# Depthwise convolution: four terms of each tile computed by TensorE, three fills placed elsewhere

## The reference, cut to what matters

```python
a = h @ pw1_w + pw1_b
u, g = jnp.split(a, 2, axis=-1)
u = u * jax.nn.sigmoid(g)
u = lax.conv_general_dilated(u, dw_w[:, None, :], (1,), [(15, 15)], ..., feature_group_count=D_MODEL) + dw_b
u = (u - mean(u)) * rsqrt(var(u) + eps) * ln_g + ln_b
return silu(u) @ pw2_w + pw2_b
```

## Time and profile before

| | us |
|---|---|
| three runs, median (lowest to highest) | 3093.72 (3091.89 to 3101.62) |
| the profiled execution | 3105.27 |
| its span, from first to last instruction | 3103.2 |
| TensorE busy | 2953.2 (95%) |
| VectorE, ScalarE, GpSimd busy | 1638.8, 1289.8, 168.0 |

### The profile page before, as it was taken

The page is one execution under the profiler, slowest core; times in us unless marked ns, Lnnn a source line. Parts: engine busy times, 40 slices in busy tenths (PEclk is TensorE's granted clock), DMA queues, the critical chain, the costliest instruction groups (busy, mean ns, idle before and its releaser), DMA issues.

```text
span 3103.2 us, 50896 instructions
## 1 busy us (share of the span) xinstructions
PE 2953.2 (95%) x17586; PEld 2524.6 (81%) x17586; DVE 1638.8 (53%) x3043; ACT 1289.8 (42%) x2511; POOL 168.0 (5%) x120
## 2 busy tenths in 40 slices
PE   7999999999999999999998868999999999989998
PEld 7979789799797997788886536788878888768998
DVE  5566775565567755532326785523334333448554
ACT  4445455455454555422323443423333323335543
POOL 0000010000000100000001760000000000000000
PEclk9999999999999999999999989999999999999999
DMA  7556265565562655532324761423324333241553
GB/s 248 187 163 211 82 204 188 155 203 186 160 211 82 207 190 168 169 98 95 102 75 167 240 217 55 136 82 108 103 70 127 95 95 105 79 143 61 167 181 99
DMA packets 239196, 443.10 MB, mean 143 GB/s; under 512 B 26416, under 2 KB 27440, under 8 KB 238384
## 3 DMA queue, kind: packets, MB, share of 16 engines
q1 hardware_dynamic: 237632, 433.47, 43.7%
q0 software_dynamic: 1392, 7.34, 0.7%
HBM read 439.65 MB, written 1.05 MB: 142 GB/s over the span
## 4 chain that ended last, share of the span: by engine, by line
PE 82%; DVE 11%; POOL 2%; issue 2%; ACT 1%; DMA 1%; SPq 0%; DVEq 0%; ACTq 0%; POOLq 0%
PE ps L749 81%; DVE low L1768 2%; POOL hidden L2382 1%; DMA raw<-weights 1%; DVE hidden L1771 1%; DVE zl L1771 1%; DVE ps L1771 1%; POOL low L2352 1%; DVE x L1774 1%; DVE hidden L1768 1%; DVE coef L2305 1%; DVE zl L1768 1%; DVE hidden L2309 1%; DVE neg_max L2105 1%; DVE hidden L2132 0%
## 5 line engine op out<-in xcount | busy, mean ns | idle before, releaser
L749 PE MATMUL ps<-zh,low 128*128 128x256 f32 (+1 forms) x4192 | 1402.6, 335 | 79.4 <-DVE low L1768 37.4
L749 PE MATMUL ps<-zl,high 128*128 128x256 f32 (+1 forms) x4192 | 1382.4, 330 | 0.0
L749 PE MATMUL ps<-zh,high 128*128 128x256 f32 (+1 forms) x4192 | 1381.5, 330 | 0.0
L1768 DVE TENSOR_TENSOR low<-raw,high 128x512 fp32r<-128x512 f32 x1276 | 844.0, 698 | 439.7 <-ACT high L1308 437.8
L1308 ACT ACTIVATE high<-raw 128x512 fp32r<-128x512 f32 x1304 | 765.5, 625 | 609.2 <-PE ps L749 508.2
L749 PEld LDWEIGHTS ps<-zh,low 128*128 128x128 f32 x4192 | 806.5, 192 | 187.3 <-issue 41.5
L749 PEld LDWEIGHTS ps<-zl,high 128*128 128x128 f32 x4192 | 807.1, 193 | 72.1 <-issue 4.8
L749 PEld LDWEIGHTS ps<-zh,high 128*128 128x128 f32 x4192 | 806.8, 192 | 69.5
L1768 DVE TENSOR_TENSOR hidden<-gated,ps 128x256 f32 (+1 forms) x176 | 91.6, 520 | 603.2 <-ACT gated L1308 603.2
L1308 ACT ACTIVATE gated<-ps 128x256 f32<-128x256 f32 (+1 forms) x176 | 81.3, 462 | 493.7 <-PE ps L749 493.6
L749 PE MATMUL ps<-high,zl 128*128 128x512 f32 (+2 forms) x544 | 196.0, 360 | 3.8 <-DVE zl L1768 3.8
(11 more groups left out here) (202 smaller groups left out, 2018.5 us busy)
## 6 DMA issues: line engine op xcount, KB each, us to landing
raw<-weights SPq DMA_DIRECT2D x1642, 256.0 KB, 3.3
hidden<-norms POOLq DMA_DIRECT2D x4, 1024.0 KB, 6.4
cst<-consts SPq DMA_DIRECT2D x1, 1829.0 KB, 12.9
x<-x_in SPq DMA_DIRECT2D x1, 1024.0 KB, 6.0
x<-tokens_in POOLq DMA_DIRECT2D x1, 1024.0 KB, 12.5
x<-ctx_in POOLq DMA_DIRECT2D x1, 1024.0 KB, 6.3
out<-hidden POOLq DMA_DIRECT2D x1, 1024.0 KB, 5.1
```

Of the source, the lines that this page charges most:

```text
L749: return nc.tensor.matmul(out, lhsT, rhs, start=first, stop=last, **kw)
L1768: return nc.vector.tensor_tensor(out, a, b, op)
```

## The change

Of every tile the last 4 terms (of the last tile the last 12) go to TensorE. Their weights come as new quarters in the stream, one for four terms, each term a 128 by 128 matrix with the term's weights on its diagonal. ScalarE and VectorE make high and low parts of a window of the tile (`window_of`), in a buffer that takes the place of `h_split` in the convolution; TensorE writes the sum of its terms into the PSUM bank (`tap_product`), and VectorE then goes on adding its own terms to it. For tile 0, TensorE uses the other bank, and its sum is added to the side sum. Side products are now 7 for each tile and 5 for the last, also for tile 0; the side sum is added to VectorE's at the end, in one more instruction. GpSimd makes all low parts of the stage from the second quarter of tile 1's second half on. The convolution has 15 fills in place of 18: the first five half tiles have none behind them, and four come at the end, the last of them behind the mean in place of a `stream(12, 2)`; one fill goes behind the first block's ple, two more to the attention. The diff, cut to its core:

```diff
-SIDES = (0, 7, 9, 9, 9, 9, 9, 13)
-LATE_FILLS = 3
+SIDES = (7, 7, 7, 7, 7, 7, 7, 5)
+TAP_QUARTERS = (1, 1, 1, 1, 1, 1, 1, 3)
+LATE_FILLS = 5
 WARM = 18
 PAD = (TAPS - 1) // 2
+WINDOW = 268
...
+def conv_order():
+
+    for t in range(KT):
+        yield "up_half", t, 0
+        if t >= 3:
+            yield "fill", t, 0
+        if t >= 1:
+            yield "taps", t - 1, 0
+        yield "up_half", t, 1
+        if t >= 2:
+            yield "fill", t, 1
+    yield "taps", KT - 1, 0
+    for _ in range(4):
+        yield "fill", KT, 0
+
+
+def taps_by_pe(n):
+
+    return 4 * TAP_QUARTERS[n]
...
-        if l == DEPTH - 1:
-            yield fills.pop()
+        yield fills.pop()
...
-            for t in range(KT):
-                for a in range(2):
+            for step, t, a in conv_order():
+                if step == "up_half":
                     yield ("up_half", ("conv", 0), (t, a), 2, False)
+                elif step == "taps":
+                    yield ("taps", ("conv", 0), t, TAP_QUARTERS[t], False)
+                else:
                     yield fills.pop()
-            yield fills.pop()
-            yield fills.pop()
...
+        elif kind == "taps":
+            parts = [np.zeros((P, taps_by_pe(t), P), np.float32)]
+            parts[0][np.arange(P), :, np.arange(P)] = inp["conv_dw_w_2"][0][TAPS - taps_by_pe(t):, t * P:t * P + P].T
+            parts = [parts[0].reshape(P, -1)]
...
+        up_at, taps_at, fill_at = {}, {}, []
+        at = 0
+        for kind, key, t, n, _ in stream():
+            if kind == "up_half":
+                up_at[t] = at
+            elif kind == "taps":
+                taps_at[t] = at
+            elif kind == "ada" and up_at:
+                fill_at.append(at)
+            if key == ("pw2", 0):
+                break
+            at += n
+        pw2_at = at
...
-                if l == DEPTH - 1:
-                    self.pe.wait_ge(res_ready, 4 * DEPTH)
+                self.pe.wait_ge(res_ready, 4 * (l + 1))
+                if l == 0:
+                    self.fill(2, 3)
+                else:
                     self.fill()
...
+            def tap_product(self, n, z0):
+
+                self.pe.wait_ge(tap_low, n + 1)
+                if n == 1:
+                    self.pe.wait_ge(taps_added, 1)
+                if n >= 2:
+                    self.pe.wait_ge(z_ready, z0 + n - 1)
+                bank, last = 5 if n == 0 else 4 + n % 2, taps_by_pe(n) - 1
+                for c0 in range(0, last, 4):
+                    h, lo = self.quarter()
+                    for i in range(4):
+                        at = slice(c0 + i, c0 + i + S)
+                        w = (h[:, i * P:i * P + P], lo[:, i * P:i * P + P])
+                        m = self.mm3(ps[:, bank, :], w, (window[:, n % 2, 0, :, at], window[:, n % 2, 1, :, at]), c0 + i == 0, c0 + i == last)
+                    self.done(m)
...
-                for n in range(KT):
-                    if n >= 2:
-                        pe.wait_ge(conv_taken, seen.now(conv_taken) + n - 1)
-                    for a in range(2):
+                z0 = seen.now(z_ready)
+                steps = list(conv_order())
+                for step, n, a in steps[:-1]:
+                    if step == "fill":
+                        self.fill(6, 7)
+                    elif step == "taps":
+                        self.tap_product(n, z0)
+                    else:
+                        if n >= 2 and a == 0:
+                            pe.wait_ge(conv_taken, seen.now(conv_taken) + n - 1)
                         self.group([(ps[:, 2 * (n % 2) + g, :], True) for g in range(2)], 512, coming=coming if n == 0 else None, halves=(a,))
-                        self.fill(6, 7)
                 seen(conv_taken, KT)
-                self.fill(6, 7)
-                self.fill(6, 7)
                 for k in range(KT):
                     self.stat(512, 0, z_ready, conv_out, k)
-                self.stream(12, 2)
+                self.fill(6, 7)
...
+                    self.take_rows()
...
-                if l == DEPTH - 1:
+                if l == 0:
+                    self.fill(2, 3)
+                else:
                     self.fill()
...
-                self.act.wait_ge(quarter_done, self.q + RING)
+                self.act.wait_ge(quarter_done, up_at[n, 1] + 2 + RING)
...
+            def window_of(self, n):
+
+                self.act.wait_ge(conv_taken, self.seen.now(conv_taken) + n + 1)
+                if n >= 2:
+                    self.act.wait_ge(quarter_done, taps_at[n - 2] + TAP_QUARTERS[n - 2] + RING)
+                wide, at = S + taps_by_pe(n) - 1, TAPS - taps_by_pe(n)
+                self.f(r(window[:, n % 2, 0, :, 0:wide]), conv_in[:, n, :, at:at + wide], ACT.Copy).then_inc(tap_high, 1)
+
             def conv(self):
                 act, seen = self.act, self.seen
                 w = c("conv_w").rearrange("p (k t) -> p k t", k=KT)
-                for n in range(2):
-                    while self.s < self.q + 2:
-                        self.next_high()
-                    self.q += 2
+                fills = iter(fill_at)
+
+                def filled():
+                    self.q = next(fills)
                     self.fill(6, 7)
-                    self.next_high()
-                    self.next_high()
-                    self.q += 2
-                    self.gate_of(n)
-                    self.fill(6, 7)
-                self.next_high()
-                self.next_high()
-                for n in range(1, KT):
-                    act.wait_ge(conv_taken, seen.now(conv_taken) + n + 1)
+
+                assert self.s == up_at[1, 1] + 1
+                self.gate_of(0)
+                self.take_rows()
+                self.window_of(0)
+                for n in range(KT):
                     for t in range(SIDES[n]):
                         at = side_before[n] + t
                         if at >= 4:
                             act.wait_ge(side_added, at - 3)
                         self.f(side[:, at % 4, :].rearrange("p (a s) -> p a s", a=2), conv_in[:, n, :, t:t + S], ACT.Copy,
                                scale=w[:, n, t:t + 1]).then_inc(side_product, 1)
-                        if n == KT - 1:
-                            if t in (2, 7):
-                                self.fill(6, 7)
-                            if t == 11:
+                        if n == 0 and t < 6 or n == KT - 1 and t == 0:
+                            self.next_high()
+                        if n >= 2 and t == 0:
+                            self.take_rows()
+                        if 2 <= n < KT - 1:
+                            if t in (1, 2, 3):
+                                self.next_high()
+                            if t == 3:
+                                filled()
+                            if t == 4:
                                 self.take_rows()
-                            continue
-                        if t == 0:
-                            self.q += 2
-                            self.fill(6, 7)
-                        if t in (1, 2):
+                    if n < KT - 1:
+                        if n:
                             self.next_high()
-                        if t == 5:
-                            self.take_rows()
-                    if n < KT - 1:
-                        self.q += 2
                         self.gate_of(n + 1)
-                        self.fill(6, 7)
-                    if n < KT - 2:
-                        self.next_high()
-                        self.next_high()
+                        if n:
+                            filled()
+                            self.next_high()
+                        self.window_of(n + 1)
+                for _ in range(3):
+                    filled()
+                    self.take_rows()
+                filled()
+                assert next(fills, None) is None
+                self.q = pw2_at
                 seen(conv_taken, KT)
                 self.root_first()
                 self.ahead()
                 for k in range(0, KT, 2):
                     act.wait_ge(dev_ready, seen(dev_ready))
                     self.f(square[:, k:k + 2, :], conv_out[:, k:k + 2, :], ACT.Square).then_inc(sq_ready, 1)
+                self.take_rows()
...
-                if l == DEPTH - 1:
+                if l == 0:
+                    self.fill(2, 3)
+                else:
...
-                def next_gate(n):
-                    self.low_by_pool(2)
-                    self.q += 2
-                    self.filled()
-                    self.low_by_pool(2)
-                    self.q += 2
-                    v.wait_ge(quarter_done, self.q + RING)
-                    gate(n)
-                    self.filled()
-
-                self.used(2)
-                self.fill(6, 7)
-                self.used(2)
+                def window_of(n):
+                    wide, at = S + taps_by_pe(n) - 1, TAPS - taps_by_pe(n)
```

(121 more changed lines are left out.)

## The result

The changed kernel took **3145.38 us** (median of 4 runs, 3140.82 to 3156.31) against 3093.28: a ratio of **1.0161, interval 1.0144 to 1.0178**, or 52 us slower. One odd execution of a later kernel, 6088.39 us in the run fast_after, is left out of that kernel's ratio. The prediction said 3119, with a range of 3098 to 3132: the right sign, half the size. The profiled execution has a span of 3154.5 us against 3103.2.

The account below looks back on a forecast made before the run. TensorE was taken as the bound, busy 2953.2 of 3103.2 us, with the convolution's tiles set by a loop of fills, loads and matmuls. Terms 15.3 + 13.5 − 3.5 = +25.3 us took the 3093.72 median to 3119, range 3098 to 3132.

Parts of the forecast that it names:

- Without a price: Buffer name, pw2's layout, moved column copy and earlier row copy: no cost, under 1 us if their cover went.
- the buffer's new name: The renamed split buffer in the convolution: listed as costing nothing, under 1 us at most.
- A fill at the first block's end: After the first block's gate stage: ScalarE's high parts delay the split of x and the next FFN, +15.3 us.
- Two late fills: In attention before the scores: two more fills at 6.2 to 7.3 us each, nothing covering them, +13.5 us.
- The convolution: Whole convolution stage: earlier start and end, most given back by the fill behind the mean, −3.5 us.
- The loop: Convolution tiles 3 to 7: fill, landing, high and low parts, matmuls, next fill; 23.8 us a tile against 22.
- the wait for the side sum: Convolution's first tile: VectorE waits 4 us for GpSimd's side sum, needed before gate 1.
- the late squares: Convolution's end: ScalarE's squares wait 6 us for pw2's eighth quarter, loaded in the moved fill, delaying the second mean.
- Rival 1: Loads behind fills: the eighth is down after 7.1 us, not 10.1; +8.5 us, 3102; chance 0.12.
- Rival 2: Convolution: VectorE is the bound and gets relief, with the fills' cost −11 us, 3082.5; chance 0.15.
- Rival 3: Convolution: side products hold back low parts in every tile, +2.5 us five times; +38 us, 3132; chance 0.05.
- Rival 4: First block's end and attention: the moved fills are hidden after all; −3.5 us, 3090; chance 0.06.

Follow-up runs that it names:

- fast_after: Changed kernel, with zh, zl and the split buffer 192 bytes further in 256 column blocks and at their old place in 512 column ones: 0.9975 of the kernel before.
- shift_only: Kernel before with 384 unused bytes behind h_split and nothing else: 1.0087 of the kernel before.
- aligned: Changed kernel with 640 unused bytes behind split_buf: 3119.73 us, 1.0087 of the kernel before.
- aligned_again: The kernel of aligned run once more, beside fills_only on one chip: 1.0064 of the kernel before.
- fills_only: Kernel before with all three moves of fills, 15 left in the convolution's loop, and no tap products on TensorE: 1.0069 of the kernel before.
- ple_only: Kernel before with one fill added at the end of the first block's ple and one fewer behind the convolution's last half: 1.0031 of the kernel before.
- late_only: Kernel before with five late fills in attention for three, and the two behind the convolution's last half left out: 1.0025 of the kernel before.
- run rate: No kernel: TensorE alone, 32 products from each of 16 sources 64 bytes apart modulo 1024, then again beside other traffic: 227.5 to 233.1 ns with 512 columns.

## Why the prediction was right, and where it failed

- **The step that failed** is in the paragraph "Without a price": "the buffer's new name". It was not a new name but 96 floats more, and they moved zh and zl by 384 bytes. I had the sizes before me, priced the step under 1 us and gave no reason for it: I took an address for something without a time. It costs 27 us on the old kernel (shift_only) and 23 to 30 on the new one (1.0161 against 1.0087 and 1.0064 for aligned; 26 by the medians). The 3 × 1536 products of the three FFNs that read zh or zl, by 5.5 to 6.6 ns, are 25 to 30.
- **A fill at the first block's end, +15.3:** measured 15.4 and 15.6, and 14.1 to 15.4 in aligned, aligned_again and fills_only. Also the steps inside held: the split started 8.4 us after the fill (forecast 8.1), behind the fifth load.
- **Two late fills, +13.5:** 12.7 from turn to scores, 12.3 and 15.4 over the stage.
- **The convolution, −3.5:** against the 282.5 us that it takes in most executions, the changed one took 277.3 to 282.9, so 0 to −5. The loop (22.2 to 23.2 for 23.8), the wait for the side sum (3.74 for 4) and the late squares were there. That −3.5 lies inside is in part luck: it was worked out against a trace whose convolution was 8 us long, and against that same trace the change gained 7.8. Its reason was half right, too: I put a gain on the new order, and fills_only has the same from three fills fewer. VectorE's lighter load brought nothing, as written.
- **The sum without the failed step** was +25.3, and aligned measured +20 and +27.
- **Rival 1** (loads as fast as the fastest) falls: the first block's term would have been 12.9. **Rival 2** (VectorE gets relief, 3082.5) falls: VectorE waits 1.95 to 4.99 us before each tile from the second on. **Rival 3** (3132) is the nearest to the time, but for a cause that isn't there: the loop would have been 2.5 us longer than forecast, and it is shorter. **Rival 4** falls by ple_only and late_only.
- The trace of before had bad luck of its own, the convolution 8 us long. Subtracting its 11.5 us as a whole was a fair guess.
- The chances: 0.71 for slower was fair. The range was too narrow, because it was made of the costs that I had listed, and the unknown one was not among them.

## What to carry to other kernels

When a change resizes a buffer, compute what moves behind it, and compare the start to start time of the untouched inner products in both traces before explaining anything else. When the sum of the changed parts is right and the total is not, cut both traces at the same landmarks and look where nothing was changed. And price a moved piece of work by what the same queue pays at its new place: three fills cost 28 us where they arrived and gave back 7 where they left.

## What the runs showed of the hardware

In the run rate a product of 128x128 weights with 512 columns of 4 bytes starts every 227.5 to 233.1 ns at the full granted clock, by the distance modulo 256 bytes of its two operands; with 256 columns it is 119.7 to 113.1, in another order, so that the best distance for the one (0) is the worst for the other (with 256 columns only the moving operand was moved). Distances other than multiples of 64 bytes weren't tried, nor whether the place in PSUM counts. Why the order turns round with the number of columns stays open.

The Trainium skill, "SBUF — State Buffer", section "Operand start alignment", says that an operand may start at any multiple of its element size, and says of itself that this is about legality, not speed. The runs here add the speed: all 16 places of the run rate are multiples of 4 bytes and ran, and between them lie 2.5% at 512 columns and 6% at 256.
